# Branch and output projections of the second block as split fp32r products, with group norm sums taken chunk by chunk

## The reference, cut to what matters

```python
h = h + 0.5 * swiglu(rmsnorm(h, ffn1_norm), ffn1_w_in, ffn1_w_out)
xn = rmsnorm(h, mix_norm)
z = xn @ w_in                                   # mixer inputs and two gates
y_a = rwkv7_mixer(...)                          # 256 x 512
y_b = mlstm_mixer(...)                          # 256 x 512
u = sigmoid(g_a) * (y_a @ br_a) + sigmoid(g_b) * (y_b @ br_b)
h = h + u @ w_out
h = h + 0.5 * swiglu(rmsnorm(h, ffn2_norm), ffn2_w_in, ffn2_w_out)
```

```python
y = head_standardize(y, 64e-5) * gn_w + gn_b    # (y - mean) / sqrt(var + eps), per token and head
y_a = (y + bonus) * g
```

## Time and profile before

| | us |
|---|---|
| median of 3 runs | 2533.22 (2527.1 to 2536.44) |
| the profiled execution's own time | 2522.09 |
| its span, first to last instruction | 2520.2 |
| PE busy | 2403.6 (95%) |
| VectorE, ScalarE, GpSimd busy | 1263.0, 1013.7, 234.1 |
| mean granted TensorE clock | 0.981 |

### The profile page before, as it was taken

The page is one execution under the profiler, slowest core; times in us unless marked ns, Lnnn a source line. Parts: engine busy times, 40 slices in busy tenths (PEclk is TensorE's granted clock), DMA queues, the critical chain, the costliest instruction groups (busy, mean ns, idle before and its releaser), DMA issues.

```text
span 2520.2 us, 50452 instructions
## 1 busy us (share of the span) xinstructions
PE 2403.6 (95%) x20892; PEld 2211.4 (88%) x20892; DVE 1263.0 (50%) x1988; ACT 1013.7 (40%) x1608; POOL 234.1 (9%) x199
## 2 busy tenths in 40 slices
PE   7989999999999799899999999999999999989998
PEld 3756899999976699899998888999999988988998
DVE  1053365565424355465477543555555567543554
ACT  3154444444334434343356521433434455422333
POOL 0000000000000000010015420100100135311000
PEclk9999999999999899999999899999999998999999
DMA  6156554455326454354432213554455332214542
GB/s 266 67 201 234 194 180 178 161 194 179 118 101 229 175 189 183 122 191 179 162 134 102 84 62 125 211 190 178 153 189 183 109 130 72 85 68 180 195 176 98
DMA packets 65076, 392.46 MB, mean 156 GB/s; under 512 B 7216, under 2 KB 7344, under 8 KB 27440
## 3 DMA queue, kind: packets, MB, share of 16 engines
q1 hardware_dynamic: 63792, 383.81, 41.8%
q10 hardware_dynamic: 864, 5.16, 0.5%
q0 software_dynamic: 288, 1.57, 0.2%
HBM read 389.46 MB, written 1.05 MB: 155 GB/s over the span
## 4 chain that ended last, share of the span: by engine, by line
PE 82%; DVE 5%; POOL 4%; issue 4%; ACT 3%; DMA 2%; POOLq 0%; SPq 0%; DVEq 0%; ACTq 0%
PE ps L1906 20%; PE ps L1907 19%; PE ps L1908 19%; PE ps L1992 6%; POOL t_lo L560 3%; PE ps L2007 2%; PE ps L2474 2%; PE ps L2306 2%; PE ps L2512 2%; DMA ring_a<-in_wa 2%; POOL h_lo L538 1%; PE ps L2447 1%; PE ps L1876 1%; PE ps L2022 1%; DVE work L1341 1%
## 5 line engine op out<-in xcount | busy, mean ns | idle before, releaser
L1906 PE MATMUL ps<-h_hi,w_hi 128*128 128x256 f32 x2464 | 701.4, 285 | 7.4 <-DVE mod L1189 2.9
L1907 PE MATMUL ps<-h_lo,w_hi 128*128 128x256 f32 x2464 | 698.0, 283 | 0.0
L1908 PE MATMUL ps<-h_hi,w_lo 128*128 128x256 f32 x2464 | 697.9, 283 | 0.0
L1906 PEld LDWEIGHTS ps<-h_hi,w_hi 128*128 128x128 f32 x2464 | 473.7, 192 | 12.4 <-issue 4.6
L1907 PEld LDWEIGHTS ps<-h_lo,w_hi 128*128 128x128 f32 x2464 | 473.7, 192 | 0.1
L1908 PEld LDWEIGHTS ps<-h_hi,w_lo 128*128 128x128 f32 x2464 | 473.7, 192 | 0.0
L1261 DVE TENSOR_TENSOR w_lo<-ring_a,w_hi 128x1024 fp32r<-128x1024 f32 x308 | 366.4, 1231 | 24.3 <-ACT w_hi L643 24.2
L1906 PE MATMUL ps<-hid_hi,d_hi 128*128 128x256 f32 x1232 | 348.7, 283 | 0.0
L1907 PE MATMUL ps<-hid_lo,d_hi 128*128 128x256 f32 x1232 | 348.7, 283 | 0.0
L1908 PE MATMUL ps<-hid_hi,d_lo 128*128 128x256 f32 x1232 | 348.6, 283 | 0.0
L1295 DVE TENSOR_TENSOR hid<-sg,ps 128x256 f32<-128x256 f32 x154 | 64.9, 422 | 545.4 <-ACT sg L675 545.3
(11 more groups left out here) (292 smaller groups left out, 3275.0 us busy)
## 6 DMA issues: line engine op xcount, KB each, us to landing
ring_a<-in_wa SPq DMA_DIRECT2D x282, 1024.0 KB, 4.8
ring_d<-in_wd SPq DMA_DIRECT2D x154, 512.0 KB, 5.2
work<-in_wa SPq DMA_DIRECT2D x6, 1024.0 KB, 21.9
work<-in_small POOLq DMA_DIRECT2D x2, 768.0 KB, 6.2
c<-in_c ACTq DMA_DIRECT2D x1, 1175.0 KB, 10.7
work<-in_c ACTq DMA_DIRECT2D x1, 1088.0 KB, 5.9
x<-in_x ACTq DMA_DIRECT2D x1, 1024.0 KB, 15.1
work<-in_ctx ACTq DMA_DIRECT2D x1, 1024.0 KB, 19.5
```

The lines of the kernel that those rows point to most:

```text
L1906: nc.tensor.matmul(out, hi, to_hi, start=start, stop=False, skip_group_check=True)
L1907: nc.tensor.matmul(out, hi, to_lo, start=False, stop=False, skip_group_check=True)
L1908: return nc.tensor.matmul(out, lo, to_hi, start=False, stop=stop, skip_group_check=True)
```

## The change

- The 16 tiles per layer of `br` and `w_out` (NB = 16, index e) go through the same tile buffers: ScalarE's `round_b(e)`, GpSimd's rest in two halves, TensorE's `split_product`. `round_b(0)` and `round_b(1)` come behind the last two gates' `empty_gate`; from e = 2 on each waits until TensorE has done tile e - 2 (`b_done`). The ring is now freed by GpSimd.
- y_b, y_a and `umix` are split as well. y_b: ScalarE's copy `yb_hi` after each chunk's `empty_gate`, VectorE's `yb_lo` before each chunk's nu. y_a: in two halves. `umix`: tile by tile (`u_hi`, `u_lo`) into `h_hi` and `h_lo`.
- The group norm's sums, centring and squares are taken per chunk on 128x256 (`chunk_sums`), those of chunk c - 1 ahead of chunk c's nu. The bonus, gn_b and gate are combined at chunk 0. The transposes become 32 products of 64x64 with `eye` that lay both heads on their partitions, so VectorE reads the result from PSUM and ScalarE's two copies go.
- TensorE does `branch(1, 1)` behind the last gate tile instead of ahead of the transposes.
- The norm of the second feed-forward part squares its pieces between the roundings of the output tiles.

The diff, cut to its core:

```diff
...
 hid_hi, hid_lo = (sb(n, 2, T, dtype=F32R) for n in ("hid_hi", "hid_lo"))
 SPLIT = 3 * 2 * 2 * KD * P + 2 * 2 * T
+
+def four_tiles(v):
+    return v.rearrange("p k c -> p (k c)").rearrange("p (j t) -> p j t", t=T)
+
+yb_hi, yb_lo = four_tiles(w_lo[:, 1, 0]), four_tiles(w_lo[:, 0, 0])
+ya_hi, ya_lo = four_tiles(d_hi[:, 0]), four_tiles(d_lo[:, 0])
...
+        for e in range(NB):
+            slot, c = (e + 1) % 2, chunk0[f"br{l}"] + e // 2
+            pool.wait_ge(b_hi, l * NB + e + 1)
+            for part in range(2):
+                k = slice(part * KD // 2, (part + 1) * KD // 2)
+
+                done = b_half if part == 0 else a_used if e % 2 else b_even
+                nc.gpsimd.tensor_tensor(t_lo[:, slot, k], ring_a[:, c % 2, e % 2, k],
+                                        t_hi[:, slot, k].bitcast(F32), ALU.subtract).then_inc(done, 1)
...
+            else:
+                round_b(t + 2 - NT2)
...
+        def round_b(e):
+
+            c = chunk0[f"br{l}"] + e // 2
+            if e % 2 == 0:
+                act.wait_ge(a_loaded[c % 2], 16 * (c // 2 + 1))
+            if e < 2:
+                act.wait_ge(t_done, (l + 1) * NT2 + e - 1)
+            else:
+                act.wait_ge(b_done, l * NB + e - 1)
+            nc.scalar.copy(t_hi[:, (e + 1) % 2], ring_a[:, c % 2, e % 2]).then_inc(b_hi, 1)
...
             for t in gates_at("chunk", c):
                 empty_gate(t)
+            act.wait_ge(ml_v, MVS.at(f"yb{c}", l))
+            nc.scalar.copy(yb_hi[:, c, :], yb[:, c, :]).then_inc(yb_h, 1)
         empty_gate(gates_at("y", 0)[0])
-        act.wait_ge(rw_v, RV.at("s2", l))
+        act.wait_ge(rw_v, RV.at(f"s2{NC_ - 1}", l))
         nc.scalar.activation(small_y[:, 4, :], small_y[:, 3, :], ACT.Sqrt, bias=const("eps_gn"),
...
-        act.wait_ge(rw_p, RP.at("yT", l))
-        src = ps[0:64, 0:4, :].rearrange("p b (u c) -> p (b u) c", c=P)
-        for h in range(2):
-            ins = nc.scalar.copy(units(tmp)[h * 64:h * 64 + 64, :, :], src[:, :, h * 64:h * 64 + 64])
-        ins.then_inc(rw_a, 1)
         empty_gate(gates_at("y", 1)[0])
 
-        act.wait_ge(br_free, (l + 1) * KD)
-        norm(("ffn2", l, 0), x[:, :, :], 4 + 2 * l, ready=3 * l + 1)
+        for i in range(2):
+            js = slice(2 * i, 2 * i + 2)
+            act.wait_ge(ya_part, 2 * l + i + 1)
+            nc.scalar.copy(ya_hi[:, js, :], ya[:, js, :]).then_inc(ya_h, 1)
+        for n in range(KD):
+            round_b(n + 2)
+            act.wait_ge(br_free, l * KD + n + 1)
+            nc.scalar.copy(h_hi[:, n, :], umix[:, n, :]).then_inc(u_hi, 1)
+
+        def rounds(i):
+            if i < PIECES - 1:
+                round_b(KD + 2 + 2 * i)
+                round_b(KD + 3 + 2 * i)
+            if i == PIECES - 2:
+                round_a(4 + 2 * l, 0)
+
+        norm(("ffn2", l, 0), x[:, :, :], ready=3 * l + 1, between=rounds)
         round_h(split_id[("ffn2", l, 0)])
         ffn(4 + 2 * l)
...
+        yps = ps[:, 2:4, :].rearrange("p b (j u t) -> p (b j) u t", t=HD, u=NC_)
+        stat = lambda i, c: small_y[:, i, :].rearrange("p (j u) -> p j u", u=NC_)[:, :, c:c + 1]
...
+        def chunk_sums(c):
+
+            dve.wait_ge(ch_p, CP.at("y", l * NC_ + c))
+            nc.vector.reduce_sum(stat(0, c), yps[:, :, c, :], AX_X).then_inc(rw_v, 1)
+            v(f"s1{c}", l)
+            nc.vector.tensor_scalar(stat(1, c), stat(0, c), -1.0 / HD, None, ALU.mult).then_inc(rw_v, 1)
+            v(f"ym{c}", l)
+            nc.vector.tensor_tensor(chunk_of(yy, c), yps[:, :, c, :], wide_stat(1, c), ALU.add)\
+                .then_inc(rw_v, 1)
+            v(f"yc{c}", l)
+            nc.vector.tensor_tensor(chunk_of(yq, c), chunk_of(yy, c), chunk_of(yy, c), ALU.mult)\
+                .then_inc(rw_v, 1)
+            v(f"yq{c}", l)
+            nc.vector.reduce_sum(stat(3, c), chunk_of(yq, c), AX_X).then_inc(rw_v, 1)
...
+            if c == 0:
+                v("bon", l)
+                for j in range(QT):
+                    ins = nc.vector.scalar_tensor_tensor(bon[:, j, :], bon[:, j, :], vcol(f"gn_b{l}", j),
+                                                         gg[:, j, :], ALU.add, ALU.mult)
+                ins.then_inc(rw_v, 1)
+            else:
+                chunk_sums(c - 1)
+            dve.wait_ge(yb_h, step + 1)
+            nc.vector.tensor_tensor(yb_lo[:, c, :], yb[:, c, :], yb_hi[:, c, :].bitcast(F32), ALU.subtract)\
+                .then_inc(yb_l, 1)
             dve.wait_ge(ch_p, CP.at("u", step))
             nc.vector.tensor_scalar(nu[:, :, c * CHUNK:(c + 1) * CHUNK],
...
+        chunk_sums(NC_ - 1)
         dve.wait_ge(rw_a, RA.at("ysd", l))
...
-        nc.vector.tensor_tensor(units(yy), units(yy), wide_stat(5), ALU.mult).then_inc(rw_v, 1)
-        dve.wait_ge(rw_a, RA.at("yT", l))
+        nc.vector.tensor_tensor(units(yy), units(yy), small_y[:, 5, :][:, :, None].to_broadcast([P, UNITS, HD]),
+                                ALU.mult).then_inc(rw_v, 1)
+        dve.wait_ge(rw_p, RP.at("yT", l))
         for j in range(QT):
-            ins = nc.vector.tensor_scalar(tmp[:, j, :], tmp[:, j, :], vcol(f"gn_w{l}", j),
-                                          vcol(f"gn_b{l}", j), ALU.mult, ALU.add)
+            ins = nc.vector.scalar_tensor_tensor(tmp[:, j, :], wide(0)[:, j, :], vcol(f"gn_w{l}", j),
+                                                 gg[:, j, :], ALU.mult, ALU.mult)
         ins.then_inc(rw_v, 1)
...
+        v("yg", l)
+        for i in range(2):
+            js = slice(2 * i, 2 * i + 2)
+            nc.vector.tensor_tensor(ya[:, js, :], tmp[:, js, :], bon[:, js, :], ALU.add).then_inc(ya_part, 1)
+
+
+        for i in range(2):
+            js = slice(2 * i, 2 * i + 2)
+            dve.wait_ge(ya_h, 2 * l + i + 1)
+            nc.vector.tensor_tensor(ya_lo[:, js, :], ya[:, js, :], ya_hi[:, js, :].bitcast(F32), ALU.subtract)\
+                .then_inc(ya_l, 1)
...
+        def rest_u(n):
+            dve.wait_ge(u_hi, l * KD + n + 1)
+            nc.vector.tensor_tensor(h_lo[:, n, :], umix[:, n, :], h_hi[:, n, :].bitcast(F32), ALU.subtract)\
+                .then_inc(u_lo, 1)
...
+            dve.wait_ge(b_done, l * NB + n + 1)
             nc.vector.tensor_tensor(umix[:, n, :], ps[:, 4 + n % 2, 0:T], gate_a[:, n, :], ALU.mult)\
                 .then_inc(br_part, 1)
             nc.vector.tensor_tensor(xs[:, n % 2, :], ps[:, 4 + n % 2, T:2 * T], gate_b[:, n, :], ALU.mult)\
                 .then_inc(br_part, 1)
+            if n:
+                rest_u(n - 1)
             dve.wait_ge(br_part, 2 * r + 2)
             nc.vector.tensor_tensor(umix[:, n, :], umix[:, n, :], xs[:, n % 2, :], ALU.add).then_inc(br_free, 1)
+        rest_u(KD - 1)
...
+            dve.wait_ge(b_done, l * NB + KD + 2 * n + 2)
...
+        def rest_here(e, part):
+            if part == 0:
+                pe.wait_ge(b_half, l * NB + e + 1)
+            elif e % 2:
+                pe.wait_ge(a_used, chunk0[f"br{l}"] + e // 2 + 1)
+            else:
+                pe.wait_ge(b_even, (l * NB + e) // 2 + 1)
+
...
+            slot, (y_hi, y_lo) = (n + 1) % 2, ((ya_hi, ya_lo), (yb_hi, yb_lo))[part]
+            rest_here(n, part)
             for k in range(QT):
-                mm = nc.tensor.matmul(ps[:, 4 + n % 2, part * T:(part + 1) * T],
-                                      ring_a[:, c % 2, n % 2, part * QT + k, :], y[:, k, :],
-                                      start=(k == 0), stop=(k == QT - 1))
+                if n == 0 and part == 0 and k % 2 == 0:
+                    pe.wait_ge(ya_l, 2 * l + k // 2 + 1)
+                mm = split_product(ps[:, 4 + n % 2, part * T:(part + 1) * T],
+                                   (t_hi[:, slot, part * QT + k, :], t_lo[:, slot, part * QT + k, :],
+                                    y_hi[:, k, :], y_lo[:, k, :]),
...
-        pe.wait_ge(ml_v, MVS.at(f"yb{QT - 1}", l))
-        chunk_here(chunk0[f"br{l}"], chunk0[f"br{l}"] % 2)
+        pe.wait_ge(yb_l, (l + 1) * QT)
         pe.wait_ge(ch_v, CV.at("s", l * NC_ + NC_ - 1))
         branch(0, 1)
-        branch(1, 1)
 
         pe.wait_ge(rw_v, RV.at("yn", l))
         for u in range(UNITS):
-            j, c = u // NC_, u % NC_
-            mm = nc.tensor.transpose(ps[0:64, u // 4, u % 4 * P:(u % 4 + 1) * P],
-                                     yy[:, j, c * CHUNK:(c + 1) * CHUNK], ident)
+            for h in range(2):
+                rows = slice(h * HD, h * HD + HD)
+                mm = nc.tensor.matmul(out_unit(0, u, h), unit(yy, u, h), const("eye")[rows, :],
...
         tile(gates_at("y", 1)[0], bank=6)
 
-        pe.wait_ge(rw_v, RV.at("ya", l))
+        branch(1, 1)
         for n in range(KD):
-            c = chunk0[f"br{l}"] + n // 2
             if n >= 2:
-                if n % 2 == 0:
-                    chunk_here(c, c % 2)
                 pe.wait_ge(br_free, l * KD + n - 1)
-                branch(n, 1)
...
-                        pe.wait_ge(br_free, l * KD + k + 1)
```

(56 more changed lines are left out.)

20 lines of the change are left out of this document (5 added, 15 removed).

## The result

| | us |
|---|---|
| before, median of 6 runs | 2529.64 (2522.07 to 2536.44) |
| after, median of 6 runs | 2551.4 (2548.1 to 2560.65) |
| ratio | 1.0104 [1.0084, 1.0123] |
| the profiled execution of after, its span | 2560.65, 2558.4 |
| mean granted TensorE clock, before and after | 0.981, 0.970 |

The change makes the kernel 1.0% slower by the ratio; the two medians differ by 21.8 us, 0.9%. The page of after gives no hint of where: the chain that ended last is 82% TensorE, as before, and GpSimd's share is the same 4%.

The account below looks back on a forecast made before the run. The prediction took TensorE as the bound (82% of the chain). Its terms, 18.1 + 0.6 + 6.0 - 1.8 = +22.9 us on a median of 2533.2, gave 2556, with an 8 in 10 range of 2536 to 2571.

Parts of the forecast that it names:

- The chunk loop's wait and hold: RWKV chunks: nu waits behind `yb_hi` and a `yb_lo` held by GpSimd; 2.26 us a chunk, 18.1 in all.
- 1.4 without the hold: RWKV chunks: TensorE's delay if GpSimd does not hold up `yb_lo`; 1.4 us a chunk, 11.2 in all.
- The clock in the chunks: RWKV chunks: longer gaps lower TensorE's clock in half the chunks, 1.5 us each; +6.0, bounds 0 and 13.6.
- The way from Y to the first tile: Behind the chunk loop: two TensorE gaps over 4 us; `branch(0, 0)` starts at 19.3 instead of 15.1.
- Y: Zero of the prediction's times behind the chunk loop: start of the group norm, 1515.84 in layer 0 before.
- The 16 tiles: Branch and output projections: 14 tiles from 23.3 at 2.95 us each, ending at Y + 66.0, 69.0 with two clock falls.
- The norm: Norm behind the output projection: only the last piece is left after the last tile; gain 0.9 us per layer, 1.8.
- tail and norm together: Everything behind the chunk loop, both layers: +0.6 us to the projections' end, -1.8 for the norm.
- no hold, no falls: Rival, chunk loop: `yb_lo` is not held and the clock stays up; +10 us, 2543; chance 0.24.
- the hidden wait: Rival, chunk loop and tiles: chunk wait costs nothing, tiles run at TensorE's pace; -14 us, 2519; chance 0.08.
- GpSimd was not the bound: Judges a rival on the tiles: GpSimd becomes the bound, 3.35 us a tile; 2567, or 2575; chance 0.12.
- the 19 us of cheaper products: The 16 tiles: split products at 0.36 instead of 0.434 us; 9.5 less per layer, if TensorE never waits.

Follow-up runs that it names:

- the second set: The changed kernel run and profiled once more, unaltered, on the same chip as its variants: 2554.24 us, ratio 1.0122.
- the filled kernel: Changed kernel plus six unread fp32 products of constants ahead of TensorE's wait for nu in each chunk: 2545.56 us, ratio 1.0092.
- the one with the gates first: Changed kernel with TensorE doing both last gate tiles ahead of the small products and first branch products: 2538.31 us, ratio 1.0063.
- the kernel with the wait alone: Changed kernel with the `yb_lo` subtraction behind nu, VectorE still waiting for `yb_hi` ahead of nu: 2531.78 us, ratio 1.0033.
- the moved copy: Changed kernel with ScalarE's copy `yb_hi` ahead of the chunk's `empty_gate` instead of behind it: 2528.78 us, ratio 1.0017.
- the copy, the gate and the root moved: Changed kernel with `yb_hi` copied ahead of `empty_gate`, both last gate tiles first, and ScalarE's root ahead of `round_b(0)`: 2505.68 us, ratio 0.9931.

## Why the prediction was right, and where its terms were off

I had predicted 2556 us, 22.9 more than before; it is 2551.4 beside a before of 2529.64, and 30.0 more in the second set. Direction and mechanism hold. That the first total came so near is in part luck, as the sum below shows. Point by point:

- **The chunk loop's wait and hold: right.** Predicted 2.26 us a chunk, 18.1 in all; the timeline shows 2.23 and the filled kernel 17.6. Each step came as written, `yb_lo` ready to start 1.66 behind the sigmoid and ended at 2.92 (measured 2.94). Reading as a hold to the end of GpSimd's half, and not as a slow instruction, gave this. "1.4 without the hold" was also borne out: 1.03 for the wait, plus 0.42 for an unheld subtraction.
- **The clock in the chunks: the term was mis-sized.** Predicted 3.0 a layer, a fall in half of the chunks; measured 5.5 to 5.7 in three of four loops and 3.9 in the fourth, 9.5 for the kernel in the second profile against 6.0. The step that failed is "a fall in half of the chunks, 1.5 us each": in layer 0 of the first profile three of four chunks had one, of 1.5 (4.57 against 3.06), 2.7 (6.33 against 3.65) and 1.5 (5.19). Over the three profiles with this loop (both of after, and the one with the gates first) 17 of 24 gaps were followed by slow sums, 1.3 to 2.7 us each. I had also treated gap and clock as separate risks; the kernel with the wait alone (a gap of 1.56, no fall) shows that the subtraction ahead of nu decided both.
- **The way from Y to the first tile: mechanism right, size short.** The two gaps came, of 4.06 and 4.42 us, ended by `t_lo`. The end of tile 0 was predicted at 20.8 plus two falls of 1.5, 23.8; it was 24.9. The falls were 1.7 (0.42 of 4.11) and 2.2 (0.43 of 5.20), 0.9 more than taken.
- **The 16 tiles: right but for half a microsecond.** Output tiles are 5.76 us a pair, 2.88 each, as TensorE's end of the range has it, and branch tiles 2.9 to 3.0 but for the third, which ends 4.3 behind the second. That is the hand-over that I had put at 1.1 (23.3 against 22.2). The pair with the last `umix` took 7.7, a stall of 1.9 where I had 1.4. The end came at Y + 70.4 for 69.0.
- **The norm: right in layer 0.** From the last addition to the sums read it is 2.3 us instead of 3.2, 0.9 less as predicted; in layer 1 it is 2.1 instead of 2.6, 0.6 less. Layer 0:

```profile
1608.15 0.69 DVE L1896 TENSOR_TENSOR x<-x,ps 128x512 f32<-128x512 f32 x1 [5.07 <-PE ps L1987]
...
1610.45 0.37 ACT L648 COPY nrt<-ps 128x256 f32<-128x256 f32 x1 [0.73 <-PE ps L1955]
```

- **Sum.** By the second profile: 17.6 (18.1 predicted) + 9.5 (6.0) + 1.4 (-1.2, tail and norm together) = 28.5 against 22.9. The first set's medians differ by 21.8 and its ratio's interval is 21 to 31 us, so that the total looked better than its terms: that is luck, for the terms are 5.6 us short, 3.5 of it by the clock in the chunks. The rivals: "no hold, no falls" fell in both its parts, the hidden wait is what the moved copy makes true, and GpSimd was not the bound (37.03 busy of 45.45, no tile over 3.0 but the third and the one pair).
- **What I did not see** is that both losses were of order only. I had called the 19 us of cheaper products all that can be gained if TensorE never waits, and treated the waits as given; with the copy, the gate and the root moved the kernel is 18.8 us below before, by its trace 1.7 of it the norm.

## To carry to other kernels

A wait put ahead of an operation on the path costs all that is queued ahead of its releaser on the other engine: put the releasing copy where that engine is idle (here one moved instruction gave back 25 us) before judging the change that needs it. Price a gap of TensorE together with the clock behind it: here 2.2 us more of gap a chunk brought 1.0 to 1.4 us of slow clock a chunk with it. Where a buffer is handed over between two kinds of tiles, let TensorE have work from other buffers for as long as one rounding and one rest take.

## What was not expected of the hardware

- Behind gaps of 1.56 us, one a chunk, the granted clock stayed at 1.00 in the windows of both layers. Behind gaps of 2.75 in the same loop it read 0.52 and 0.67 over the next sums; but 7 of 24 such gaps had no slow sums behind them, and in the second profile of after the first two gaps of layer 0 had none where those of layer 1 had. What decides which gap is followed by a fall no run here tells.
- Two executions of the same instructions reach S of layer 0 at different times, 1492.27 and 1487.24 in the two profiles of after. Differences of stages inside one profile were good to a few tenths, those of whole spans only to several microseconds.
- The table load ahead of the root at 1542.21 ends at 1543.49 and the root starts at 1543.50: again no pause between them, as in the earlier trace rows.
